# Attention output computed transposed for two query tiles at a time, in a hybrid decoder block

## The chip, the cores and the metric

The kernel runs on one core of one Trainium2 chip. The metric is the device time of one execution in microseconds (us); less is better. The engines' names are those of the profile: PE is TensorE (PEld its weight loads), DVE is VectorE, ACT is ScalarE, POOL is GpSimd, and SP is the sync engine, whose queue issues every DMA here.

## What is computed

One decoder block for 1024 tokens of width 1024, in float32. A normed input is projected; two kinds of attention with heads of width 64 run on the projections; their outputs are projected, gated and summed, projected again and added to the input; then comes a squared-ReLU MLP of width 4096 and a last norm. The part that matters:

```python
# 8 "fox" heads, causal over all 1024 keys, F = cumsum(log_sigmoid(fa + b))
s = q @ k.T * scale + F_q - F_k            # masked above the diagonal
oa = softmax(s) @ v
# 12 dilated heads: groups of 4 with dilation 1, 4, 16; blocks of own and previous keys
m = max(s); p = exp(s - m); denom = sum(p); lse = m + log(denom)
o_g = (p / denom) @ v
ob = sum_g softmax_g(lse)[g] * o_g         # mixture over the three groups
mixed = sigmoid(ga) * (oa @ w_branch_a) + sigmoid(gb) * (ob @ w_branch_b)
```

## The kernel before

Every float32 product is split: an operand is stored as a rounded part ("hi") and the rest ("lo", by a DVE subtraction), and two or three matmuls in the type fp32r are summed. All five engines run programs of their own, in an order written out by hand, and meet at semaphores.

**Units and steps.** After a start of 71 us the attention runs in ten units of two heads: `N_DIL` = 6 dilated units (two for each dilation), then `N_FOX` = 4 fox units. A unit has `STEPS` = 16 steps, numbered G in all: eight query tiles of 128 tokens times the unit's two heads (head `s % 2`, tile `s // 2`). The number of key tiles n of a step is 1 or 2 in a dilated unit (all 1 with dilation 16) and i + 1 in fox tile i, so 1 to 8. Between the two kinds lies the mixture of the dilated groups ("the join", L989 to L1027), and after the last unit come the branch projections, the gates and the MLP, which no longer concern the change except at their start.

**PE's step G** (`mixer_steps`, L962) is: `scores(G)` (L892, queries stationary, keys moving, both parts of q, a bank of up to four key tiles at a time); a third of the step's share of the next unit's input projections (`project_part`, L882; 128 x 512 matmuls, 144 in a unit as a rule, 96 in the first and last fox unit); `transposes(G - 1)` of the probabilities (L919, one for a key tile); the rest of the projections; `out_transpose` every second step (L931); and `values(G - 2)` (L938). In `values` a transposed tile of probabilities, 128 keys by 128 queries, is stationary, and 128 columns of values (64 hi, 64 lo) move. There are two matmuls for a key tile, since the probabilities have two parts. The result has queries on partitions; the half from the values' lo part is added, both are divided by the row sum, and the two heads' results lie side by side in `o_nat` until PE transposes them.

**DVE's step G** (L1835): `outs(G - 3)` (L1807), `maxes(G)` (L1783, adds the bias and takes the row maximum of the scores in PSUM), one job of the side work, `probs_lo(G - 1)` (L1794), `inverses(G - 1)` (L1802, a reciprocal), `q_tile(G + 2)` (L1765, two instructions), in step 1 of a unit `values_lo`, then the other jobs (splitting of weights, rotary embedding, `k_stack`).

**ACT's step G** (L1358): evacuation of a finished projection when there is one, `out_store` every second step (L1345, waits for `out_transpose`), `out_part(G - 3)` (L1337), `q_tile(G + 2)` (L1300, two instructions), `exps(G)` (L1321), `probs_hi(G - 1)` (L1329), then now and then a weight split or `k_stack`.

`values(G)` waits with `after(pe, on_done, G)` until DVE has read the result of the step before, since both lie in one bank. `scores(G)` waits for the queries of step G, which DVE makes two steps earlier (three buffers):

```python
pe.wait_ge(q_lo, 2 * G + 2)                 # L900, in scores(G)
after(pe, exp_done, G - 1)                  # L901
after(pe, on_done, G)                       # L943, in values(G)
if G < last and G + 2 < STEPS * MIX:        # L1848, in DVE's step G
    q_tile(G + 2)
```

**The join** needs the log of the row sums: ACT takes Ln of them (L1408), DVE subtracts the stored negative maxima (L1869), PE transposes the result to rows and, when ACT and DVE have put the tokens in natural order (L1409, L1871), back again (L997, L1003). DVE and ACT form the weights of the mixture (L1873 to L1888).

**SP** issues DMAs in order (L572 to L589): weight chunks, each behind a wait for its buffer, and the biases of the fox heads, broadcast from a row in DRAM to 128 partitions (L559).

Of the kernel before, what the change touches and what calls it, by code (L numbers as in the profile page):

```python
# [32 lines left out]
P = 128  # L33
# [25 lines left out]
PRIME = 1  # L59
STEPS = 16  # L60
MIX = N_DIL + N_FOX
# [92 lines left out]
def column(G):  # L154

    t, s = divmod(G, STEPS)
    if t >= N_DIL:
        return G
    return (((t // 2) * 8 + s // 2) * 2 + t % 2) * 2 + s % 2
# [14 lines left out]
def tiles_of(G):  # L174
    return key_tiles(G // STEPS, G % STEPS // 2)

# [11 lines left out]
def tile_tokens(ap, t, i):  # L188

    d = dil_of(t)  # L190
    if d in (None, 1):
        return ap[:, i * P:(i + 1) * P]
    v = ap.rearrange("p (l r) -> p r l", r=d)
    if d == 4:
        return v[:, i // 2, (i % 2) * P:(i % 2 + 1) * P]
    return v[:, 2 * i:2 * i + 2, :]


def tile_view(ap, t):

    return ap.rearrange("p (r l) -> p r l", r=2) if dil_of(t) == 16 else ap
# [20 lines left out]
def build(nc, x, g_attn, w_in, b_forget, w_branch, w_out, g_mlp, w_up, w_down, g_final, rope, f_rows, x_mid, hidden, out):  # L222
# [8 lines left out]
    with ExitStack() as ctx:  # L231
# [19 lines left out]

        up_b = [at(f"up_b{j}", [P, 2, 4, HALF], F32R, 64 + 16 * j) for j in range(3)]
# [23 lines left out]
        o_nat = sb("o_nat", [P, 2, P], F32)  # L276
        o_part = sb("o_part", [P, 2, HD], F32)
        negmax = sb("negmax", [P, STEPS * MIX], F32)
        rowsum = sb("rowsum", [P, STEPS * MIX], F32)
        rowinv = sb("rowinv", [P, STEPS * MIX], F32)  # L280
# [13 lines left out]
        v_nat = work[:, 4 * 1024:6 * 1024].rearrange("p (t h s d) -> p t h s d", t=8, h=2, s=2)  # L294
        q_st = work[:, 6144:6912].rearrange("p (b s c) -> p b s c", b=3, s=2)
        pt = work[:, 8 * 1024:12 * 1024].rearrange("p (b s c) -> p b s c", b=2, s=2)
# [13 lines left out]
        def ot_bank(i):  # L310

            return PS[1][:, HALF:HALF + P] if i < 8 * N_DIL else pso[:, 256:256 + P]

        def score_bias(G, n):

            t, s = divmod(G, STEPS)
            if t >= N_DIL:
                return fbias[t % 2][:, s % 2, 0:n * P]
# [4 lines left out]
        lse_nat = tmp[:, 6, 0:96].rearrange("p (g c) -> p g c", g=3)  # L323
        top = tmp[:, 6, 96:128]
        lrow = [tmp[0:4, 0, :], tmp[0:4, 1, :], tmp[0:4, 3, :]]
# [4 lines left out]
        def probs(G):  # L330

            if G < STEPS * N_DIL:
                return tmp[:, 6, (G % 2) * 256:(G % 2 + 1) * 256]
# [2018 lines left out]
```

## Time and profile before

| | us |
|---|---|
| median of 3 runs (1696.52 to 1700.22) | 1698.19 |
| the profiled execution's own time | 1698.49 |
| its span, first to last instruction | 1696.7 |
| six dilated units, 71 to 394 | 323 |
| the join, 394 to 425 | 31 |
| four fox units, 425 to 710 | 285 |
| everything after, 710 to the end | 986 |
| PE busy, share of the span | 94% |

The profiled execution lies 0.3 us above the median, and 1.8 us of it are outside the span. Busy time counts the union of an engine's instructions; the ends of matmuls are modelled, so the start of one matmul to the start of the next is the better price of it.

### The profile page before, as it was taken

The page shows a single profiled execution, that of the slowest core. Times are in us where ns is not written, and L with a number is a line of the kernel's source. Part 1 is how long each engine was busy: PE and PEld are TensorE (multiplying, and loading weights), DVE is VectorE, ACT ScalarE, POOL GpSimd, SP SyncE. Part 2 cuts the span into 40 slices and gives each one's busy share as a digit, 9 for nine tenths or more (in the row PEclk, how much of TensorE's full clock was granted, in tenths as well). Part 3 has the DMA queues.
Part 4 walks back from the last instruction along what each step waited for, and adds up shares of the span by engine and source line. Part 5 has one row for each costly group of instructions (what it writes and reads, how often), then busy time and mean ns, then how long its engine had stood idle before and what let it go on. Part 6 is the DMA issues. An engine that isn't in the chain of part 4 may idle for free. (4 is left out here: it accounts for less than half of the span.)

```text
span 1696.7 us, 22852 instructions
## 1 busy us (share of the span) xinstructions
PE 1592.8 (94%) x7832; PEld 1305.4 (77%) x7832; DVE 1114.5 (66%) x2167; ACT 831.1 (49%) x1715; POOL 4.1 (0%) x20
## 2 busy tenths in 40 slices
PE   5998998898799999999999999999999889999997
PEld 5777777675688887788888887888888667777786
DVE  5688788875666666622213667666666777777776
ACT  6566777783556666611113445344333444444441
POOL 0000000000000000000000000000000000000000
PEclk9999999999899999999999999999999999999998
DMA  5210110010010200011112533444444783444412
GB/s 174 87 38 26 26 38 26 26 38 13 14 50 14 63 26 10 16 53 47 49 53 71 149 101 92 157 154 143 153 165 156 238 283 135 153 137 137 143 38 100
DMA packets 160828, 152.45 MB, mean 90 GB/s; under 512 B 6856, under 2 KB 126664, under 8 KB 160592
## 3 DMA queue, kind: packets, MB, share of 16 engines
q1 hardware_dynamic: 160720, 151.06, 27.9%
q8 instruction: 61, 1.00, 0.2%
q14 instruction: 47, 0.39, 0.1%
HBM read 113.25 MB, written 37.78 MB: 89 GB/s over the span
## 5 line engine op out<-in xcount | busy, mean ns | idle before, releaser
L877 PE MATMUL ps<-hspl,wsp 128*128 128x512 f32 x1536 | 426.0, 411 | 8.3 <-ACT tmp L1290 6.7
L877 PEld LDWEIGHTS ps<-hspl,wsp 128*128 128x128 f32 x1536 | 268.0, 191 | 54.9 <-ACT tmp L1290 8.5
L1170 PE MATMUL ps<-dn_b,a_hi 128*128 128x512 f32 x896 | 279.6, 393 | 19.6 <-DVE keep L1957 13.9
L833 PE MATMUL ps<-hspl,wsp 128*128 128x512 f32 x960 | 223.2, 393 | 0.6 <-ACT keep L1356 0.6
L1170 PEld LDWEIGHTS ps<-dn_b,a_hi 128*128 128x128 f32 x896 | 167.8, 189 | 61.3 <-issue 26.1
L833 PEld LDWEIGHTS ps<-hspl,wsp 128*128 128x128 f32 x960 | 181.6, 190 | 38.5 <-issue 0.8
L1170 PE MATMUL ps<-dn_b,a_lo 128*128 128x512 f32 x448 | 175.7, 392 | 0.0
L1798 DVE TENSOR_TENSOR work<-ps,work 128x128 fp32r<-128x128 f32 (+3 forms) x192 | 84.4, 454 | 102.7 <-ACT work L1334 100.3
L949 PEld LDWEIGHTS ps<-work 128*128 128x128 f32 x856 | 112.6, 192 | 47.6 <-issue 37.6
L1326 ACT ACTIVATE tmp<-ps,negmax 128x128 f32<-128x128 f32 (+7 forms) x160 | 87.5, 547 | 122.8 <-DVE negmax L1791 121.0
L949 PE MATMUL ps<-work 128*128 128x128 f32 x856 | 122.9, 276 | 21.1 <-DVE o_nat L1813 20.0
L1957 DVE TENSOR_TENSOR keep<-keep,ps 128x512 f32<-128x512 f32 (+1 forms) x144 | 101.5, 713 | 38.3 <-PE ps L1170 23.6
L1170 PE MATMUL ps<-up_b,a_hi 128*128 128x512 f32 x384 | 119.6, 393 | 3.7 <-DVE up_b L1957 2.6
L1309 ACT ACTIVATE work<-tmp 64x128 fp32r<-64x128 f32 x320 | 113.3, 354 | 5.9
L1770 DVE SCALAR_TENSOR_TENSOR work<-tmp,work 64x128 fp32r<-64x128 f32 x320 | 101.5, 317 | 9.3 <-ACT work L1309 1.8
L1546 ACT ACTIVATE keep<-keep 128x512 f32<-128x512 f32 x64 | 40.5, 633 | 125.9 <-DVE keep L2129 42.8
L1170 PEld LDWEIGHTS ps<-dn_b,a_lo 128*128 128x128 f32 x448 | 84.7, 189 | 18.0
L916 PE MATMUL ps<-work 128*128 128x256 f32 (+3 forms) x384 | 89.2, 327 | 3.1 <-issue 2.1
L1957 DVE TENSOR_TENSOR dn_b<-dn_raw,dn_b 128x1024 fp32r<-128x1024 f32 x56 | 67.2, 1221 | 37.1 <-ACT dn_b L1562 37.1
L1948 DVE TENSOR_TENSOR wsp<-raw,wsp 128x1024 fp32r<-128x1024 f32 x18 | 22.0, 1223 | 105.8 <-ACT wsp L1454 105.8
L1993 DVE TENSOR_TENSOR a_lo<-a_raw,a_hi 128x1024 fp32r<-128x1024 f32 (+1 forms) x66 | 81.3, 1234 | 11.1 <-ACT a_hi L1512 10.9
L1170 PEld LDWEIGHTS ps<-up_b,a_hi 128*128 128x128 f32 x384 | 72.6, 190 | 19.7 <-DVE up_b L1957 3.1
(202 smaller groups left out, 2486.2 us busy)
## 6 DMA issues: line engine op xcount, KB each, us to landing
hidden<-keep SPq DMA_DIRECT2D x112, 256.0 KB, 2.2
dn_raw<-hidden SPq DMA_DIRECT2D x56, 512.0 KB, 6.0
raw<-in_w_in SPq DMA_DIRECT2D x47, 512.0 KB, 3.8
a_raw<-in_w_up SPq DMA_DIRECT2D x36, 256.0 KB, 3.1
a_raw<-in_w_down SPq DMA_DIRECT2D x32, 256.0 KB, 3.0
spare<-in_w_down SPq DMA_DIRECT2D x32, 256.0 KB, 4.6
spare<-in_w_up SPq DMA_DIRECT2D x28, 256.0 KB, 3.1
keep<-in_x SPq DMA_DIRECT2D x8, 512.0 KB, 7.1
```

The lines of the kernel that those rows point to most:

```text
L833: ins = pe.matmul(ps[:, cols], w(wp, k), mv(mp, k)[:, cols], start=(k == 0 and n == 0), stop=(k == ks - 1 and n == 2))
L877: ins = pe.matmul(psp(u, g), wsp[c % 2][:, wp, k * P:(k + 1) * P], hspl[:, mp, k, cols], start=(n == 0), stop=(n == 23), skip_group_check= ...
L916: ins = pe.matmul(oo, lt, rh, start=(m == 0), stop=(m == len(ops) - 1), skip_group_check=True)
L949: ins = pe.matmul(o, pt[:, G % 2, part, n * P:(n + 1) * P], v_nat[:, j, s % 2, :, :].rearrange("p s d -> p (s d)"), start=(part == 0 and n ...
L1170: ins = pe.matmul(o, a_part(n, j, wp, k), b_block(n, j, mp, k), start=(first and k == 0 and m == 0), stop=(k == ks - 1 and m == 2), skip_g ...
L1309: act.activation(tile_view(q_st[dst:dst + 64, G % 3, 0, :], t), tile_tokens(q_raw(t)[row:row + 64], t, s // 2), ACT.Copy, scale=-QSCALE).t ...
L1326: act.activation(probs(G)[:, 0:n * P], psc[G % 2][:, 0:n * P], ACT.Exp, bias=negmax[:, c:c + 1], scale=-1.0, accum_out=rowsum[:, c:c + 1]) ...
L1546: act.activation(u, u, ACT.Square).then_inc(signal, 1)
L1770: dve.scalar_tensor_tensor(out=tile_view(q_st[dst:dst + 64, G % 3, 1, :], t), in0=tile_tokens(q_raw(t)[row:row + 64], t, s // 2), scalar=- ...
L1798: dve.tensor_tensor(pt[:, G % 2, 1, a * P:b * P], PS[2][:, (u % 2) * HALF:(u % 2) * HALF + (b - a) * P], pt[:, G % 2, 0, a * P:b * P].bitc ...
L1957: return dve.tensor_tensor(out, a, b, op)
L1993: dve.tensor_tensor(a_lo_t[q % 2][b][:], src[:], a_hi_t[q % 2][b][:].bitcast(F32), ALU.subtract).then_inc(a_lo, 1)
```

## The change

The steps of a unit are ordered anew: `query_tile(s)` is `2 * (s // 4) + s % 2` and `head_of(s)` is `s // 2 % 2`, so that steps 2B and 2B + 1 are two neighbouring query tiles of one head, a block B (eight in a unit). The values become stationary (128 keys by 64 hi and 64 lo columns) and the probabilities of both tiles move, 256 columns where both tiles use a key tile and 128 where only one does. The result has the head's width on partitions, so `out_transpose` and `out_store` are gone, and DVE writes the sum of the two halves to its place. It isn't divided by the row sum. In the dilated units the weights of the mixture are formed from maxima and row sums without Ln (`mix_e`, `mix_r`); in the fox units a unit's 16 columns of reciprocals are transposed, stored to a new DRAM tensor `r_rows`, read back broadcast to 64 partitions for each head (`inv_wide`, in the buffer of the raw values), and DVE multiplies the whole unit's output once (`normalise`). `values(B)` runs at the end of PE's step 2B + 3. Queries are made in blocks of 256 columns, two ACT and two DVE instructions for two steps, in two buffers. `scores(2B)` waits for `q_lo` of both halves, the second of which DVE makes in step 2B - 1. Outputs have two banks in the dilated units and one in the fox units.

```diff
-    if t >= N_DIL:
-        return G
-    return (((t // 2) * 8 + s // 2) * 2 + t % 2) * 2 + s % 2
+def query_tile(s):
+
+    return 2 * (s // 4) + s % 2
+
+
+def head_of(s):
+
+    return s // 2 % 2
+
+
+def block_keys(B):
+
+    t, b = divmod(B, BLOCKS)
+    keys = [[j for j, _ in key_tiles(t, b // 2 * 2 + e)] for e in range(2)]
+    both = [j for j in keys[0] if j in keys[1]]
+    order = [(j, (0, 1)) for j in both]
+    order += [(j, (e,)) for e in range(2) for j in keys[e] if j not in both]
+    return min(keys[0] + keys[1]), order
 
 
...
+                             inv_rows[0:STEPS, :]).then_inc(inv_stored, 16)
+                sp.wait_ge(inv_stored, 16 * (f + 1))
+                sp.wait_ge(vt_done, 2 * min(N_DIL + f + 2, MIX))
+                for h in range(2):
+                    sp.dma_start(inv_wide[h * HD:(h + 1) * HD, :],
+                                 r_rows[2 * f + h:2 * f + h + 1, :].broadcast_to((HD, S))).then_inc(inv_in, 16)
+
             for i in range(4):
...
-                pe.wait_ge(q_lo, 2 * G + 2)
+                pe.wait_ge(q_lo, 2 * (G // 2) + 2)
                 after(pe, exp_done, G - 1)
+                query = q_st(G // 2)[:, :, G % 2 * P:(G % 2 + 1) * P]
                 ps = psc[G % 2]
...
+            def inverse_rows(f):
+
+                pe.wait_ge(inv_done, f + 1)
+                pe.wait_ge(on_done, BLOCKS * (N_DIL + f + 1) - 1)
+                pe.transpose(inv_bank, rowinv[:, f * STEPS:(f + 1) * STEPS], ident[:])
+
+            def values(B):
+                t, b = divmod(B, BLOCKS)
+                pe.wait_ge(pt_lo, units_before(2 * B + 2))
                 pe.wait_ge(v_lo, 2 * t + 2)
-                after(pe, on_done, G)
-                if t >= N_DIL:
-                    pe.wait_ge(ote_done, (G - 1) // 2)
-                o = pso[:, (s % 2) * P:(s % 2 + 1) * P]
-                for part in range(2):
-                    for n, (j, _) in enumerate(tiles):
-                        ins = pe.matmul(o, pt[:, G % 2, part, n * P:(n + 1) * P],
-                                        v_nat[:, j, s % 2, :, :].rearrange("p s d -> p (s d)"),
-                                        start=(part == 0 and n == 0), stop=(part == 1 and n == len(tiles) - 1))
+                after(pe, on_done, B if t >= N_DIL else B - 1)
+                base, keys = block_keys(B)
+                o = o_bank(B)
+                for n, (j, es) in enumerate(keys):
+                    cols = slice(es[0] * P, (es[-1] + 1) * P)
+                    for part in range(2):
+                        moving = pt(B, part)[:, j - base, es[0]:es[-1] + 1, :].rearrange("p e c -> p (e c)")
+                        ins = pe.matmul(o[:, cols], v_nat[:, j, 2 * (b % 2):2 * (b % 2) + 2, :].rearrange("p a d -> p (a d)"),
+                                        moving, start=(part == 0 and (n == 0 or len(keys[0][1]) == 1)),
+                                        stop=(part == 1 and n == len(keys) - 1), skip_group_check=True)
                 ins.then_inc(pv_done, 1)
...
-                    late = G if first else G - 1
-                    if late % 2 == 0 and late - 4 >= first:
-                        out_transpose((late - 4) // 2)
-                    if first <= G - 2 < last:
-                        values(G - 2)
+                    if G % 2 and first <= G - 3 < last:
+                        if G % STEPS == 1 and first:
+                            inverse_rows(G // STEPS - N_DIL - 1)
+                        values((G - 3) // 2)
                     if G % STEPS == 1 and G < last:
...
+            def query_hi(B, n):
+
+                t, b = divmod(B, BLOCKS)
+                if n == 0:
+                    act.wait_ge(raw_out, 6 * t + 4)
+                    if t < N_DIL:
+                        act.wait_ge(roped, 16 * t + 16)
+                    after(act, qk_done, 2 * B - 2)
+                row = 64 * (b % 2)
+                dst = row if n == 0 else 64 - row
+                act.activation(pair_view(q_st(B)[dst:dst + 64, 0, :], t), pair_tokens(q_raw(t)[row:row + 64], t, b // 2),
+                               ACT.Copy, scale=-QSCALE).then_inc(q_hi, 1)
...
+            def inverse_rows(f):
+
+                act.wait_ge(pv_done, BLOCKS * (N_DIL + f + 1))
+                after(act, inv_stored, 16 * f)
+                act.copy(inv_rows[0:STEPS, :], inv_bank).then_inc(inv_out, 1)
+
+            def out_part(B):
+
+                row = 64 * (B % 2)
+                act.wait_ge(pv_done, B + 1)
+                after(act, on_done, B - 1)
+                act.copy(o_part[row:row + 64, :], o_bank(B)[64 - row:P - row, :]).then_inc(op_done, 1)
...
-                    late = G if first else G - 1
-                    if late % 2 and first <= late - 5 < last:
-                        out_store((late - 5) // 2)
-                    if first <= G - 3 < last:
-                        out_part(G - 3)
-                    if G < last and G + 2 < STEPS * MIX:
-                        q_tile(G + 2)
+                    if G % 2 == 0 and first <= G - 4 < last:
+                        if s == 2 and first:
+                            inverse_rows(t - N_DIL - 1)
+                        out_part((G - 4) // 2)
+                    if G < last and G // 2 + 1 < BLOCKS * MIX:
+                        query_hi(G // 2 + 1, G % 2)
                     if G < last:
                         exps(G)
...
-            act.activation(rowsum[:, 0:96], rowsum[:, 0:96], ACT.Ln).then_inc(ln_ok, 1)
+            act.activation(mix_e, mix_e, ACT.Exp).then_inc(lexp_ok, 1)
...
+            def query_lo(B, n):
+                t, b = divmod(B, BLOCKS)
+                row = 64 * (b % 2)
+                dst = row if n == 0 else 64 - row
+                dve.wait_ge(q_hi, 2 * B + n + 1)
+                dve.scalar_tensor_tensor(out=pair_view(q_st(B)[dst:dst + 64, 1, :], t),
+                                         in0=pair_tokens(q_raw(t)[row:row + 64], t, b // 2), scalar=-QSCALE,
...
+            def inverses(f):
+                dve.wait_ge(exp_done, STEPS * (N_DIL + f + 1))
+                cols = slice(f * STEPS, (f + 1) * STEPS)
+                dve.reciprocal(rowinv[:, cols], fox_stat[:, 1, cols]).then_inc(inv_done, 1)
+
+            def outs(B):
+                t, b = divmod(B, BLOCKS)
+                row = 64 * (b % 2)
+                dst = og[:, t // 2, (t % 2) * 1024:(t % 2 + 1) * 1024] if t < N_DIL else keep[:, (t - N_DIL) * 1024:(t - N_DIL + 1) * 1024]
+                dve.wait_ge(op_done, B + 1)
+                dve.tensor_tensor(pair_tokens(dst[row:row + 64], t, b // 2), pair_view(o_bank(B)[row:row + 64, :], t),
+                                  pair_view(o_part[row:row + 64, :], t), ALU.add).then_inc(on_done, 1)
+
+            def normalise(f):
+                dve.wait_ge(inv_in, 32 * (f + 1))
+                dve.wait_ge(on_done, BLOCKS * (N_DIL + f + 1))
+                o = keep[:, f * 1024:(f + 1) * 1024]
+                dve.tensor_tensor(o, o, inv_wide, ALU.mult).then_inc(norm_ok, 1)
...
+                if t > N_DIL and s == 11:
+                    jobs.append(lambda: normalise(t - N_DIL - 1))
...
-                    if first <= G - 3 < last:
-                        outs(G - 3)
+                    if G % 2 == 0 and first <= G - 4 < last:
+                        outs((G - 4) // 2)
...
-                        inverses(G - 1)
-                    if G < last and G + 2 < STEPS * MIX:
-                        q_tile(G + 2)
+                        if first and G > first and s == 0:
+                            inverses(t - N_DIL - 1)
+                    if G < last and G // 2 + 1 < BLOCKS * MIX:
+                        query_lo(G // 2 + 1, G % 2)
...
+            link(dve.tensor_tensor(mix_r, mix_e, sum_nat, ALU.mult))
+            link(dve.tensor_tensor(top, mix_r[:, 0, :], mix_r[:, 1, :], ALU.add))
+            link(dve.tensor_tensor(top, top, mix_r[:, 2, :], ALU.add))
...
 
-            for k in range(6):
+            for n, k in enumerate(BR_ORDER):
                 src = keep[:, k * 1024:(k + 1) * 1024] if k < 4 else ob[:, (k - 4) * 1024:(k - 3) * 1024]
-                dve.wait_ge(br_hi, k + 1)
+                if k == N_FOX - 1:
+                    normalise(k)
```

## Rows read from the trace of the kernel before

**Rows 1.** The page's first part: busy time of the engines.
```profile
PE 1592.8 (94%) x7832; PEld 1305.4 (77%) x7832; DVE 1114.5 (66%) x2167; ACT 831.1 (49%) x1715; POOL 4.1 (0%) x20
```
**Rows 2.** By stage: window, length, busy PE, PEld, DVE, ACT, POOL, granted clock, DMA share, GB/s.
```profile
71.00:394.00 323.00, 294.05 (x1576) 234.53 (x1575) 257.16 (x832) 232.15 (x705) 0.00 (x0) 0.99 0.11 30
425.00:710.00 285.00, 267.32 (x1664) 225.57 (x1662) 181.35 (x515) 176.68 (x487) 0.00 (x0) 0.96 0.10 28
...
568.00:639.00 71.00, 69.83 (x440) 59.47 (x438) 45.47 (x130) 45.77 (x125) 0.00 (x0) 1.00 0.15 38
639.00:710.00 71.00, 65.21 (x430) 54.55 (x428) 42.51 (x128) 41.63 (x121) 0.00 (x0) 0.99 0.05 14
```
**Rows 3.** Waits from 71 to 394 us: who waited for whom, total us, times, longest.
```profile
PE ps L949 <- DVE o_nat L1813: 18.4, 27, 1.7
```
**Rows 4.** Timeline of PE in a fox unit: start, us, instruction.
```profile
622.51 2.09 PE L877 MATMUL ps<-hspl,wsp 128*128 128x512 f32 x8
624.44 1.45 PE L949 MATMUL ps<-work 128*128 128x128 f32 x12
625.73 1.14 PE L916 MATMUL ps<-work 128*128 128x512 f32 x4
```
**Rows 5.** Timeline of PE in a dilated unit: two 128 x 256 matmuls, then the second alone.
```profile
129.99 0.48 PE L916 MATMUL ps<-work 128*128 128x256 f32 x2
...
130.19 0.28 PE L916 MATMUL ps<-work 128*128 128x256 f32 x1
130.31 0.40 PE L877 MATMUL ps<-hspl,wsp 128*128 128x512 f32 x1
```
**Rows 6.** Groups of instructions by line and shape, 71 to 710 us: xcount | busy us, mean ns.
```profile
L1309 ACT ACTIVATE work<-tmp 64x128 fp32r<-64x128 f32 x316 | 112.0, 355 | 5.8
L1770 DVE SCALAR_TENSOR_TENSOR work<-tmp,work 64x128 fp32r<-64x128 f32 x316 | 100.3, 317 | 8.1 <-ACT work L1309 0.7
L1342 ACT ACTIVATE o_part<-ps,rowinv 128x64 f32<-128x64 f32 x160 | 51.9, 324 | 17.2 <-PE ps L949 16.2
L1813 DVE SCALAR_TENSOR_TENSOR o_nat<-ps,rowinv,o_part 128x64 f32<-128x64 f32 x160 | 45.0, 281 | 39.3 <-ACT o_part L1342 37.3
L1356 ACT COPY keep<-ps 128x128 f32<-128x128 f32 x80 | 25.7, 321 | 26.9 <-PE ps L949 24.9 <-PE ps L936 1.6
L1798 DVE TENSOR_TENSOR work<-ps,work 128x256 fp32r<-128x256 f32 x60 | 25.4, 423 | 18.6 <-ACT work L1334 18.1
L1805 DVE RECIPROCAL rowinv<-rowsum 128x1 f32<-128x1 f32 x160 | 24.5, 153 | 0.0
L1334 ACT CAST work<-ps 128x256 fp32r<-128x256 f32 x60 | 21.9, 365 | 0.0
L1791 DVE CUSTOM_DVE_ANT_0 ps<-ps,dil_bias 128x256 f32<-128x256 f32 x44 | 18.6, 423 | 0.0
L1326 ACT ACTIVATE tmp<-ps,negmax 128x256 f32<-128x256 f32 x52 | 24.7, 474 | 38.4 <-DVE negmax L1791 37.5
```
**Rows 7.** Timeline at the end of the last fox unit, two steps with eight key tiles.
```profile
694.34 1.22 DVE L1791 CUSTOM_DVE_ANT_0 ps<-ps,fbias 128x1024 f32<-128x1024 f32 x1
...
698.69 1.23 DVE L1791 CUSTOM_DVE_ANT_0 ps<-ps,fbias 128x1024 f32<-128x1024 f32 x1
...
710.44 13.71 PE L833 MATMUL ps<-hspl,wsp 128*128 128x512 f32 x48 [0.56 <-ACT keep L1356]
```
**Rows 8.** Timeline of the end of the dilated units and the join.
```profile
390.60 0.28 DVE L1798 TENSOR_TENSOR work<-ps,work 128x128 fp32r<-128x128 f32 x1
...
395.88 2.78 PE L997 MATMUL ps<-ident,rowsum 128*4 128x128 f32 x24 [0.49 <-DVE rowsum L1869]
...
404.76 1.28 ACT L1412 ACT_TABLE_LOAD   x1
```
**Rows 9.** Timeline of SP's queue: a row tensor stored to DRAM and read back broadcast.
```profile
56.58 0.48 SPq L581 DMA_DIRECT2D f_rows<-keep  x1
60.16 1.76 SPq L559 DMA_DIRECT2D fbias<-f_rows  x4
```

More of the change, by code:

```diff
@@ L174, in tiles_of @@
 def tiles_of(G):
-    return key_tiles(G // STEPS, G % STEPS // 2)
+    return key_tiles(G // STEPS, query_tile(G % STEPS))
 def units_of(G):
@@ L321, in score_bias, with stat @@
             return dil_bias[:, 2 - n:2, :].rearrange("p a c -> p (a c)")
-        lse_nat = tmp[:, 6, 0:96].rearrange("p (g c) -> p g c", g=3)
-        top = tmp[:, 6, 96:128]
-        lrow = [tmp[0:4, 0, :], tmp[0:4, 1, :], tmp[0:4, 3, :]]
+        stat_nat = tmp[:, 1, 0:192].rearrange("p (w x c) -> p w x c", w=2, c=4)
+        neg_nat, sum_nat = (tmp[:, 1, 96 * w:96 * w + 96].rearrange("p (g c) -> p g c", g=3) for w in range(2))
+        mix_e = tmp[:, 1, 192:288].rearrange("p (g c) -> p g c", g=3)
+        mix_r = tmp[:, 1, 288:384].rearrange("p (g c) -> p g c", g=3)
+        top = tmp[:, 1, 384:416]
+        lrow = [tmp[0:8, 0, :], tmp[0:8, 1, :], tmp[0:8, 3, :]]
+        inv_wide = tmp[:, 5, :]
+        def stat(G, w):
+            t, s = divmod(G, STEPS)
+            if t >= N_DIL:
+                c = (t - N_DIL) * STEPS + head_of(s) * 8 + query_tile(s)
+                return fox_stat[:, w, c:c + 1]
+            c = t % 2 * 2 + head_of(s)
+            return dil_stat[:, t // 2 * 8 + query_tile(s), w, c:c + 1]
         def q_raw(t):
@@ L962, in mixer_steps @@
             def mixer_steps(first, last):
-                for G in range(first, last + 4):
+                for G in range(first, last + 2):
                     if G < last:
@@ L1274, in raw_evacuate @@
                 elif g == 2:
-                    after(act, q_lo, 2 * STEPS * (u - 1))
+                    after(act, q_lo, 2 * BLOCKS * (u - 1))
+                    if u == N_DIL + 1:
+                        act.wait_ge(comb_ok, 1)
                 elif g == 4:
                     after(act, vt_done, 2 * u)
+                    after(act, norm_ok, u - 1 - N_DIL)
                     if u < N_DIL:
@@ L1896, in _ @@
                 dst = ob[:, pair * 1024:(pair + 1) * 1024]
-                one = dst if g == 0 else tmp[:, 6, :]
+                one = dst if g == 0 else tmp[:, 3, :]
                 dve.tensor_tensor(one, PS[pair][:], og[:, g, pair * 1024:(pair + 1) * 1024], ALU.mult).then_inc(spr_out, 1)
```

241 lines of the change are left out of this document (102 added, 139 removed).

## The prediction

> **What bounds the kernel now.** The page's head comes first: PE is busy for 94% of the span, DVE for 66% and ACT for 49% [rows 1], so a matmul saved in a full stage is time saved. The division by stage comes next, because the change touches only 71 to 425 us and the start of what follows [rows 2]. In the third fox unit, 568 to 639 us, PE is busy 69.8 of 71 us: work bounds it. In the fourth, 639 to 710, with 96 projections in place of 144, it is 65.2 of 71. In the dilated units PE is busy only 294 of 323 us, and the waits show why: PE stood idle 18.4 us before `values`, in 27 waits, for DVE's `outs` of the step before [rows 3].
>
> **The price of a matmul** is read from starts. Twelve 128-column matmuls of `values` take 624.44 to 625.73, 0.108 us each; eight with 512 columns take 622.51 to 624.44, 0.24 us each [rows 4]. The columns fell to a quarter and the price only to 45%: at 128 columns something else than columns sets it. A matmul of 256 columns is followed after 0.12 us (130.19 to 130.31) [rows 5]. The first of these stretches lies in a unit with the granted clock 1.00 [rows 2], that is 2.4 GHz.
>
> **The change, part by part.**
>
> *Values on PE.* A key tile used by both tiles of a block costs four matmuls of 128 columns now, 0.43 us, and two of 256 later, 0.24: 0.19 saved. By `key_tiles` a head has 4 shared key tiles with dilation 1, 4 with dilation 4, none with 16, and 1 + 3 + 5 + 7 = 16 in fox: 32 in the dilated heads, 128 in the fox heads. That is 6.1 and 24.3 us. (Matmuls: 856 to 536.) The bounds: at worst 256 columns cost 2 x 0.108, and nothing is saved; at best they cost 0.108, and 0.21 is saved.
> *Output transposes.* 80 go. Each has 128 columns; 0.108, as above, is the bound above and nothing the bound below, since most stand behind a 512-column matmul that may hide the weight load. I take 0.06: 2.9 us of the dilated units, 1.9 of fox.
> *DVE, two steps.* Now four query instructions at 0.317, two `outs` at 0.281, two reciprocals at 0.153: 2.14 us [rows 6]. Later two queries of 64 x 256, bounded by 0.317 and twice that, and one sum. The nearest row is the 128 x 256 subtraction, 0.423; I take 0.45 and 0.42: 1.32. A step loses 0.41 us.
> *ACT, two steps.* Now 4 x 0.355 + 2 x 0.324 + 0.321 = 2.39. Later two queries, 0.36 to 0.71, and one copy like the 128 x 256 cast, 0.365 [rows 6]; with 0.47 for a query, 1.31. A step loses 0.54.
> *The wait before `values`.* It now needs outputs of one block earlier (fox) or two (dilated), read by DVE over half a step before. The 18.4 us go. What is late next is below.
> *The new wait.* `scores(2B)` needs the queries that DVE makes last in step 2B - 1, after `probs_lo(2B - 2)`; before there was a step to spare. Behind this wait stand all PE's projections and transposes, and DVE's next `maxes` waits for its scores. From the end of the scores of 2B - 1 with two key tiles: maximum 0.42 and exp 0.47 with 0.1 to 0.15 of delay behind each, `probs_hi` 0.37, `probs_lo` 0.42, queries 0.45 [rows 6], some 2.4 us, while PE has eight projections (1.93), transposes (0.2) and a block of values (0.7), 2.8. So it is covered in the dilated units, by 0.4 us; a DVE job of 0.7 in between is hidden beside exp and cast, but `k_stack` is not.
> *Dilated units:* -6.1 - 2.9 - 18.4 = -27. A check: ACT and DVE set the pace in most of the 80 steps of the first five units, and 80 x 0.41 = 33. Ends: -15, if half the wait returns as another, and -38, if all PE's idle 29 us go.
> *Fox units.* DVE's steps are a ring: maximum, exp, cast, `probs_lo`, queries, next maximum. With eight key tiles and no queries left to make it takes 694.34 to 698.69, 4.35 us [rows 7]. Without reciprocal and `outs` (about 0.25 net) and with one query instruction it is 4.5. At every even step the scores come on top, four matmuls, about 1.0, less the 0.42 of `outs` that fits in: a mean of 4.9. PE's own work there is scores 1.0, transposes 8 x 0.108, half a block's values 0.95 and twelve projections 2.9 where a unit has 144, 5.7 a step; with six projections, in a unit of 96, it is 4.2. So the two middle units are bound by PE still and save a quarter of 26.2 each, 6.6. In the first and the last the ring keeps large steps as they are, and I take 4 each. The last block's output needs one wait fewer for `outs` and no transpose: 2. Fox: -23. Ends: -12 (ring everywhere) and -30 (all of PE's saving, tail included).
> *The join.* From the last `probs_lo`, 390.60, to the first transpose of statistics at 395.88 lie two waits of `values`, a transpose, a store, a table load and Ln [rows 8]. Later: one block of values, copy, sum, beside eight projections of 1.9 us: 2.5 saved. The second table load of 1.28, at 404.76, goes as well, since exp stays loaded; a wider copy and `mix_r` add 0.4. Together -3; ends -1 and -6.
> *Row sums of fox.* `normalise` is a 1.2 us DVE job in step 11 of three units, beside PE's work; its DMAs have seven steps and more. If that cover is gone, `raw_evacuate` of the values waits in step 14. SP stands still meanwhile for the store's landing, before the next weight chunk, which has several steps of room. Only the last unit's is exposed. The store and read-back of the row tensor took 3.6 us to the next issue [rows 9]; two broadcasts of half the size follow, for which I estimate 4 to 5 us, since issuing four alone took 1.76. With ACT's copy, multiply, split and the weight split behind it, about 14 us after the last `values`. PE has its next 48 products, which took 13.3 us [rows 7], plus 1 for the last output. I take +1; ends 0 and +4.
>
> Sum: -27 - 3 - 23 + 1 = -52 against the profiled execution's 1698.5: 1646. The median of the runs shown is 0.3 lower, which changes nothing. 0.2% is 3.4 us, about what a measurement of this kernel can tell from no change.
>
> **Rivals.**
> *A, the ring binds.* The new wait and the order of DVE set the pace in most steps. For it: DVE is busy 257 of 323 us in the dilated units, and its steps have few gaps there. Against: PE is fuller than DVE in each stage [rows 2]. Then the dilated units gain 17, fox 12, the join 3: -32 and +1, 1667.
> *B, 256 columns cost 0.17.* The pair takes 129.99 to 130.31, so the first, behind a transpose, took 0.2 [rows 5], and a dearer case exists. A shared tile then saves 0.09, not 0.19: 16 us less, 1662.
> *C, pairing saves no PE time.* Columns count, not matmuls, and 256 cost twice 128, which is 0.216: 30 us less, 1676. This is what the change would be if it did not do what it says. Against it stand rows 4 and 5.
> The Trainium skill speaks for C: TensorE: Matmul & The Clock Gate, Back-to-back issue gap, has an isolated gap of N / 2.4 + 2.5 ns, 56 for 128 columns and 109 for 256. By it a shared tile costs 0.222 now and 0.218 later, and the whole pairing is worth 1 us. The trace disagrees at 128 columns, with 108 ns [rows 4]. The same page gives a weight load about 107 ns (LDWEIGHTS), which with rows 4 would make the load the bound.
> *D, the cover is better.* With less work on all three engines most of PE's idle time goes too: dilated -38, fox -28, join -4, end +1: 1629.
> *E, slower.* The wait of `scores(2B)` for `q_lo`, 80 times. It eats the gain of 52 at 0.65 us a block. With a strided query instruction at 0.6 and a rotary job of 0.69 that is not hidden, the chain of 2.4 becomes 3.3 to 3.6 against 2.8 of PE; 0.8 x 80 = 64 makes 1710. Against: most jobs stand behind the queries or beside exp.
>
> **Chances.** Forecast 0.62, A 0.16, B 0.08, C 0.03, D 0.06, E 0.05. The forecast's own spread, with the ends of its terms, is 1634 to 1658. The range takes in A and B and a part of D: 1628 to 1670. Faster 0.93, within 0.2% 0.02, slower 0.05.
>
> **What would show it.** The dilated units end after 296 us instead of 323, fox takes 262 instead of 285. `values` has 536 matmuls, those of 256 columns 0.12 us apart; 0.2 apart would be B or C. No PE wait on DVE stands before it. A wait of PE's scores on DVE's query line, over 10 us in all, means A, over 40 means E. After the last unit, a wait of PE between the 48 products and the branch products over 2 us puts the row sums wrong. PE's busy share falls in the last fox unit, not in the middle two. A granted clock well below 1.00 in a middle unit would make the prices above wrong too.

## The result, and the profile after

The changed kernel takes 1676.97 us (median of 4 runs, 1672.13 to 1678.25), the kernel before beside it 1697.36 (1696.13 to 1700.22): a ratio of 0.9872, 95% interval 0.9848 to 0.9896. It is 20 us faster. The forecast was 52, and 1676.97 lies 7 us above its range of 1628 to 1670. The profiled execution took 1677.7 us, with a span of 1675.9.

The page's first part, against [rows 1]:

```profile
PE 1552.0 (93%) x7436; PEld 1277.8 (76%) x7436; DVE 1094.3 (65%) x1775; ACT 782.0 (47%) x1396; POOL 4.1 (0%) x20
```

PE is busy for 41 us less than before, and the span is only 21 us shorter. So the work went as it should, and about half of it came back as waiting. Where is told best by the starts of the maxima on DVE, one in each of the 160 steps. The first starts at 71.7 us, and these are the distances in us:

| | 1st to 96th (dilated) | 96th to 97th (join) | 97th to 160th (fox) |
|---|---|---|---|
| before | 315.4 | 41.6 | 270.3 |
| after | 309.4 | 36.6 | 263.2 |
| gone | 6.0 | 5.0 | 7.1 |

What follows the last maximum is 3 us shorter, nearly all of it behind the attention. There the profiled executions of this document differ by up to 10 us (990 to 1000) whatever the edit, so these 3 us are not put down to the change. By stage, against [rows 2] (columns as there):

```profile
71.00:382.00 311.00, 277.09 (x1447) 228.61 (x1446) 242.11 (x587) 203.67 (x507) 0.00 (x0) 0.98 0.11 30
414.00:689.00 275.00, 241.03 (x1371) 199.60 (x1372) 173.02 (x364) 156.97 (x364) 0.00 (x0) 0.95 0.12 35
554.00:622.00 68.00, 63.73 (x373) 53.12 (x372) 43.81 (x94) 40.94 (x95) 0.00 (x0) 1.00 0.18 48
622.00:690.00 68.00, 57.12 (x337) 47.34 (x336) 40.86 (x89) 36.70 (x88) 0.00 (x0) 0.96 0.08 22
```

The third fox unit (third row) has lost 6 us of PE work, as foretold, but only 3 us of its length: PE, which was busy for 69.8 of 71 us, now stands idle for 4.3 of 68. The prediction had the busy share falling in the last fox unit alone; it fell in this middle one too. The granted clock is 1.00 here as before, so the prices of matmuls hold. The longest waits of the dilated units and of fox (engine line waited for: us in total, times, longest us) say for what:

```profile
ACT tmp L1391 <- DVE dil_stat L1848: 77.0, 84, 1.6
DVE work L1855 <- ACT work L1401: 34.0, 67, 1.1
PEld ps L982 <- DVE work L1828: 27.9, 25, 2.4
PE ps L982 <- DVE work L1828: 24.3, 23, 2.3
...
PE ps L982 <- DVE q_fox L1828: 17.5, 17, 2.6
```

Line 982 is `scores`, and L1828 the query difference on DVE. The 18.4 us ahead of `values` [rows 3] are down to 1.3, and 24.3 + 17.5 = 42 us of a new wait have come. The prediction had named this wait and taken it as covered. One of these waits, on PE and on DVE:

```profile
192.32 0.40 PE L982 MATMUL ps<-work 128*128 128x256 f32 x2
...
194.52 0.57 PE L1014 MATMUL ps<-work 128*128 128x256 f32 x4
196.11 0.44 PE L982 MATMUL ps<-work 128*128 128x128 f32 x2 [1.02 <-DVE work L1828]
```

```profile
192.15 0.42 DVE L1855 TENSOR_TENSOR work<-ps,work 128x256 fp32r<-128x256 f32 x1 [0.24 <-ACT work L1401]
192.60 0.62 DVE L1828 SCALAR_TENSOR_TENSOR work<-tmp,work 64x256 fp32r<-64x256 f32 x1
193.25 0.69 DVE L1809 TENSOR_TENSOR tmp<-tmp 128x512 f32<-128x512 f32 x1
193.86 0.42 DVE L1848 CUSTOM_DVE_ANT_0 ps<-ps,dil_bias 128x256 f32<-128x256 f32 x1
194.21 0.14 DVE L1848 DVE_READ_ACCUMULATOR2_ANT dil_stat<- 128x1 f32 x1
194.21 0.69 DVE L1811 TENSOR_TENSOR tmp<-tmp 128x512 f32<-128x512 f32 x1
195.13 0.29 DVE L1855 TENSOR_TENSOR work<-ps,work 128x128 fp32r<-128x128 f32 x1 [0.24 <-ACT work L1401]
195.46 0.60 DVE L1828 SCALAR_TENSOR_TENSOR work<-tmp,work 64x256 fp32r<-64x256 f32 x1
```

The scores of the odd step end at 192.72, but their maximum starts only at 193.86, 1.14 us later: DVE has the query of the step before and a rotary job in hand. From the maximum to the end of the next query another 2.2 us pass. So the queries come 3.34 us after the scores, and PE, with 2.37 us of work in between, waits 1.02.

### The profile page after: what moved, and what is told of

Read it like the earlier page. It is cut to its first block and busy times, and to the rows that moved or that the text cites. A ratio compares the mean times of both kernels' runs of the same rounds, so it can differ in the third digit from the quotient of the medians.

```text
span 1675.9 us, 20825 instructions
## 1 busy us (share of the span) xinstructions
PE 1552.0 (93%) x7436; PEld 1277.8 (76%) x7436; DVE 1094.3 (65%) x1775; ACT 782.0 (47%) x1396; POOL 4.1 (0%) x20
## 5 line engine op out<-in xcount | busy, mean ns | idle before, releaser
L1233 PE MATMUL ps<-dn_b,a_hi 128*128 128x512 f32 x896 | 280.0, 394 | 17.5 <-DVE keep L2022 11.8
L1233 PEld LDWEIGHTS ps<-dn_b,a_hi 128*128 128x128 f32 x896 | 168.0, 189 | 59.3 <-issue 24.1
L2022 DVE TENSOR_TENSOR keep<-keep,ps 128x512 f32<-128x512 f32 (+1 forms) x144 | 101.5, 713 | 38.2 <-PE ps L1233 24.5
L1855 DVE TENSOR_TENSOR work<-ps,work 128x128 fp32r<-128x128 f32 (+3 forms) x144 | 59.1, 420 | 72.3 <-ACT work L1401 70.2
L1391 ACT ACTIVATE tmp<-ps,fox_stat 128x128 f32<-128x128 f32 (+3 forms) x64 | 47.5, 742 | 94.9 <-DVE fox_stat L1848 94.8
L993 PE MATMUL ps<-ident,tmp 128*128 128x128 f32 x428 | 75.7, 281 | 9.7 <-issue 7.1
L1580 ACT COPY ps<-ps 128x512 f32<-128x512 f32 x46 | 26.3, 571 | 123.8 <-PE ps L1233 118.4
L1233 PE MATMUL ps<-up_t4b,a_hi 128*128 128x512 f32 x256 | 80.1, 395 | 1.2 <-ACT keep L1600 1.2
L1233 PE MATMUL ps<-up_t,a_hi 128*128 128x512 f32 x256 | 79.1, 390 | 0.0
L993 PEld LDWEIGHTS ps<-ident,tmp 128*128 128x128 f32 x428 | 55.7, 144 | 29.7 <-issue 14.2
```

Source lines behind the costliest of these rows:

```text
L993: ins = pe.transpose(PS[2][:, (u % 2) * HALF + (k - a) * P:(u % 2) * HALF + (k - a + 1) * P], probs(G)[:, k * P:(k + 1) * P], ident[:])
L1233: ins = pe.matmul(o, a_part(n, j, wp, k), b_block(n, j, mp, k), start=(first and k == 0 and m == 0), stop=(k == ks - 1 and m == 2), skip_g ...
L1391: act.activation(probs(G)[:, 0:n * P], psc[G % 2][:, 0:n * P], ACT.Exp, bias=stat(G, 0), scale=-1.0, accum_out=stat(G, 1)).then_inc(exp_do ...
L1580: act.copy(s1[q] if q < 2 else bank_b(q), bank_a(q)).then_inc(s1_ok, 1)
L1855: dve.tensor_tensor(pt_tiles(G, 1, a, b), PS[2][:, (u % 2) * HALF:(u % 2) * HALF + (b - a) * P].rearrange("p (j c) -> p j c", c=P), pt_til ...
L2022: return dve.tensor_tensor(out, a, b, op)
```

## The experiments

Each is an edit of the changed kernel unless said otherwise. The distances between maxima, in us, for all:

| | dilated | join | fox |
|---|---|---|---|
| e1_query_first | 291.3 | 38.4 | 242.5 |
| e2_both_halves_even | 308.5 | 38.2 | 256.4 |
| e3_unpaired | 310.0 | 39.1 | 275.1 |
| e4_before_late_query | 359.5 | 44.5 | 291.9 |
| e5_query_first_unpaired | 294.0 | 36.8 | 261.5 |
| e6_before_query_first | 303.6 | 41.6 | 263.2 |
| e7_third_query_buffer | 301.2 | 38.1 | 262.5 |
| e8_query_first_third_buffer | 292.8 | 36.8 | 243.6 |
| e9_values_lo_late | 309.5 | 38.3 | 250.2 |
| e10_k_stack_late | 305.9 | 38.5 | 252.6 |
| e11_longer_query | 327.0 | 38.1 | 272.9 |
| e12_query_first_longer_query | 302.3 | 38.3 | 242.4 |

**e1_query_first** puts the query behind the maximum, into the time in which DVE waits for exp and cast:

```diff
                     if G < last:
                         maxes(G)
+                    if G < last and G // 2 + 1 < BLOCKS * MIX:
+                        query_lo(G // 2 + 1, G % 2)
                     for job in jobs[:1]:
                         job()
                     if first <= G - 1 < last:
                         probs_lo(G - 1)
...
-                    if G < last and G // 2 + 1 < BLOCKS * MIX:
-                        query_lo(G // 2 + 1, G % 2)
```

> The changed kernel with one order of DVE's step changed: query_lo stands right behind maxes, ahead of the side job and of probs_lo. Nothing is left out. Theory W (the wait of scores(2B) for queries made behind probs_lo, and with it DVE's ring, ate the gain): PE's idle time in front of scores falls from about 42 us (24.3 dilated, 17.5 fox) to under 8, the query instruction of 0.4 to 0.6 us goes into a gap in which DVE waited for exp and cast, and the time falls by 25 to 40 us, to 1637 to 1652. Rival D (DVE and ACT have too much work for the step, wherever the queries stand): the idle time turns up in front of transposes and values, and the time stays within 6 us of 1677. Rival M (the moving pairs or the low granted clock are what costs): 1677 too, with the wait in front of scores gone.

Measured: 1639.65 us (1638.16 to 1641.05), ratio to before 0.9653 (0.9635 to 0.967). It is 37 us below the changed kernel, beats both kernels, and nothing tried later beats it. The wait in question, in the dilated units:

```profile
PE ps L982 <- DVE work L1828: 8.5, 10, 1.7
```

In fox it is no longer among the thirteen longest. The order of two instructions was worth more than the change.

**e2_both_halves_even** makes both halves of a block's queries in the even step (ACT and DVE), where they were made one in each:

```diff
-                    if G < last and G // 2 + 1 < BLOCKS * MIX:
-                        query_lo(G // 2 + 1, G % 2)
+                    if G < last and G % 2 == 0 and G // 2 + 1 < BLOCKS * MIX:
+                        query_lo(G // 2 + 1, 0)
+                        query_lo(G // 2 + 1, 1)
```

> The changed kernel with both halves of a block's queries made in the even step 2B (ACT and DVE), one step ahead of where the second half was made. The place behind probs_lo stays, so the wait is loosened by a step and DVE's ring keeps its length. Theory W: the idle time in front of scores falls under 10 us as well, but DVE's serial work per two steps is the same, so that less is won than with the queries moved into DVE's gap: 8 to 25 us below 1677. Rival D: 1671 to 1683.

Measured: 1670.29 us (1669.31 to 1675.17), ratio 0.9842 (0.9819 to 0.9865). That lies between the ranges of the two theories. The wait of `scores` for queries is gone, and it brings only 7 us: in the dilated units the distance from an even step's maximum to the next grew from 2.51 to 3.19 us in the mean (from an odd one it fell from 4.02 to 3.30), and PE waits elsewhere, its transposes for exp. So room alone isn't it; the length of DVE's chain fits as the rest.

```profile
DVE work L1856 <- ACT work L1401: 73.4, 107, 1.9
PEld ps L993 <- ACT tmp L1391: 37.8, 39, 2.3
```

**e3_unpaired** and **e5_query_first_unpaired** take the pairing back, in the changed kernel and in e1, with all else kept:

```diff
-                    for part in range(2):
-                        moving = pt(B, part)[:, j - base, es[0]:es[-1] + 1, :]...
+                    for e in es:
+                        for part in range(2):
+                            moving = pt(B, part)[:, j - base, e, :]
```

> The changed kernel with 128 moving columns everywhere: a shared key tile takes four matmuls again, 856 in place of 536. Nothing is left out. By the price in the trace (256 columns 0.118 us, 128 columns 0.11) this adds some 32 us of PE work, 26 of it in the fox units. Theory W: PE waits about 0.5 us a block for the queries, with half of that work standing in front of the wait, so that only a part of it reaches the end: 8 to 22 us above 1677. Rival P (PE's work sets the pace and the pairing saved all of its 31 us): 28 to 34 us above.

> The changed kernel with the query differences right behind the maxima (as in e1_query_first, 1639.65 us), and beside that every values matmul with 128 columns again (856 instead of 536). In e3 the same unpairing cost only 14 us where PE stood waiting anyway. Theory W (the wait for the queries had swallowed half of what pairing saves, and is gone here): 25 to 32 us slower than e1, 1665 to 1671, near the 30.4 of the prediction's term. Rival R (the DVE ring still sets most steps, whatever the place of the queries): no more than in e3, 8 to 18 slower, 1648 to 1657.

Measured: e3 1691.16 us (1686.05 to 1698.38), ratio 0.9961 (0.994 to 0.9982); e5 1665.33 (1663.56 to 1665.93), ratio 0.9807 (0.9787 to 0.9827). Pairing is worth some 14 us where PE waits for queries (the ten runs of e3 scatter over 12) and 26 where it doesn't. By stage, where it doesn't: 2.7 us dilated and 19.0 in fox, of 6.1 and 24.3 foretold. The rest of the 26 lies behind the attention, where e5 had the clock at half for 35 us and e1 for 20; between the first and the last maximum it was the other way, 14 us and 24.

**e4_before_late_query** gives the kernel before the lack of room that the change has: `q_tile(G + 1)` and `q_tile(G + 2)` both in the odd step, on ACT and DVE.

```diff
-                    if G < last and G + 2 < STEPS * MIX:
-                        q_tile(G + 2)
+                    for x in (G + 1, G + 2) if G % 2 and G < last else ():
+                        if x < STEPS * MIX:
+                            q_tile(x)
```

> The kernel before, with one thing of the change alone: ACT and DVE make q_tile(G + 1) and q_tile(G + 2) in the odd steps G, so that the even step's scores wait for queries made one step ahead, behind probs_lo, as in the changed kernel. Work and counts are those of before. Theory W: an idle time of PE in front of scores appears in the even steps, 20 to 50 us in all, and the time rises by 12 to 40 us over 1697. Rival D (the order alone costs nothing): within 4 us of 1697.

Measured: 1764.9 us (1759.65 to 1767.52), ratio 1.0384 (1.0358 to 1.0411). The wait is there (`scores` is L916), and the slowdown of 67 us is larger than either theory's number. A part of it is the clock, which was granted at half for 65 us between the first and the last maximum, against 27 in the kernel before; at most 19 us can come from that. The wait:

```profile
PE ps L916 <- DVE work L1771: 62.2, 52, 2.7
```

Here four query instructions stand in one step, where the change has one, so this shows that the wait can arise, not its size in the change.

**e6_before_query_first** asks what e1's edit does to the kernel before, which has room:

```diff
                         maxes(G)
+                    if G < last and G + 2 < STEPS * MIX:
+                        q_tile(G + 2)
                     for job in jobs[:1]:
...
-                    if G < last and G + 2 < STEPS * MIX:
-                        q_tile(G + 2)
```

> The kernel before with its DVE query instructions moved right behind the maxima of their step, ahead of the side job and of probs_lo; nothing else. It asks whether e1's 37 us came from the wait of the scores or from a shorter DVE chain that any kernel would gain by. Theory W (before had a step to spare for its queries, so moving them serves no wait; the chain had its gaps filled by outs and reciprocals): within 5 us of the kernel before, 1693 to 1701. Rival R (queries in the shadow of exp and cast shorten DVE's chain in every step, wait or no wait): 12 to 35 us faster, 1662 to 1685.

Measured: 1679.06 us (1678.51 to 1681.83), ratio 0.9897 (0.9876 to 0.9918). My expectation missed: 19 us go where PE didn't wait for queries. If the order is worth the same in the changed kernel, 19 of e1's 37 us have nothing to do with the change and 18 belong to it; no run shows that the two add up in this way. With the queries first on both sides, the change is worth 1679.06 - 1639.65 = 39 us; with them last, 20.

**e7_third_query_buffer** restores the room and leaves the order alone, in the dilated heads (a third buffer, each query a step earlier except at the start of a head). **e8_query_first_third_buffer** adds it to e1.

```diff
-            return (q_dil if B < BLOCKS * N_DIL else q_fox)[:, B % 2]
+            return q_dil[:, B % 3] if B < BLOCKS * N_DIL else q_fox[:, B % 2]
...
-                        query_lo(G // 2 + 1, G % 2)
+                        for q in queries_of(G):
+                            query_lo(*q)
```

> The changed kernel with the order of its instructions within a step kept, but a third query buffer in the dilated heads, and each query made one step earlier there (so scores of an even step has again a step to spare, as before the change). Fox is as it was. Theory W (the missing step of room is what costs): the 24 us of PE's scores waiting on the query line between 71 and 415 us fall to under 5, and 12 to 22 us go: 1655 to 1665. Rival R (the place of the query instructions in DVE's chain costs, not the room): the wait moves to another line and 0 to 5 us go, 1672 to 1677.

> e1_query_first with the third query buffer of e7 in the dilated heads: both remedies at once. W and R alike: in e1 8.5 us of PE's scores waiting on the query line are left in the dilated heads; they go, and 2 to 8 us with them, 1632 to 1638. If the two remedies were independent and each worth its full amount, it would be 15 or more.

Measured: e7 1668.36 us (1664.98 to 1669.67), ratio 0.9824 (0.9801 to 0.9847); e8 1642.06 (1639.79 to 1643.43), 0.967 (0.9649 to 0.9691). Both miss: e7 lies between its two theories, and e8 gains nothing where 2 to 8 us were expected. In e7 the query wait is gone from the dilated units' list and 8.2 us with it; 18 us of another wait have come, of PE's transposes for ACT's exp, which waits for the maximum:

```profile
ACT tmp L1402 <- DVE dil_stat L1861: 85.1, 84, 2.3
...
PE ps L1004 <- ACT tmp L1402: 18.3, 27, 1.7
```

So the wait of `scores` and the length of DVE's chain are two limits close together. Taking away the first uncovers the second, after 8 of 24 us. In e1 the order relieves both, and there a third buffer adds nothing (2 us slower, within the scatter): e1's last 8.5 us of the query wait go, and PE's transposes wait for exp for 15.0 us where they did for 4.7 in e1.

**e11_longer_query** and **e12_query_first_longer_query** price DVE's time in the two orders: one more instruction of 64 x 128 ahead of each query, into a scratch tensor.

```diff
                 dve.wait_ge(q_hi, 2 * B + n + 1)
+                dve.scalar_tensor_tensor(out=half(pair_view(dup_out[dst:dst + 64, :], t)),
+                                         in0=half(pair_tokens(q_raw(t)[row:row + 64], t, b // 2)), scalar=-QSCALE, ...
```

> The changed kernel, order kept, with one more DVE instruction of 64x128 (the query difference of half the columns, into a scratch tensor, 0.3 us) ahead of each query difference, so last in DVE's step: it prices an error of length of the query instruction, which I had put 0.13 us a step too short. If DVE's chain sets the pace in nearly every step: 160 x 0.3 = 48 us slower, and at least 35 (1712 to 1725). If PE sets it in most: under 20 slower (under 1697).

> The same additional instruction in e1_query_first (1639.65), where it lies behind the maxima, in the time in which DVE waits for exp and cast. If the shadow of exp and cast (0.47 + 0.15 + 0.37, less the query's 0.5) still has 0.3 us of room: 0 to 12 slower, 1640 to 1652. If not: 25 to 48 slower, 1665 to 1688.

Measured: e11 1706.18 us (1702.78 to 1707.91), ratio 1.0048 (1.0033 to 1.0063), 29 above the changed kernel and between the two numbers; e12 1648.13 (1646.93 to 1651.47), 0.9715 (0.9693 to 0.9737), 8 above e1, as expected. What was added, in e11 (line, operation, shapes, xcount | busy us, mean ns):

```profile
L1833 DVE SCALAR_TENSOR_TENSOR dup_out<-tmp,work 64x128 f32<-64x128 f32 x94 | 32.3, 343 | 2.8 <-ACT work L1378 0.5
L1833 DVE SCALAR_TENSOR_TENSOR dup_out<-tmp,q_fox 64x128 f32<-64x128 f32 x61 | 17.3, 283 | 1.4
```

With the queries last, 32.3 us in the dilated units cost 17.6, and 17.3 in fox cost 9.7: 0.55 us for each. With the queries first, 11.0 and nothing.

**e9_values_lo_late** and **e10_k_stack_late** tried to improve e1 by the same rule. The second diff is e10's, on top of e9.

```diff
+                    if s == 2 and G < last:
+                        values_lo(t)
                     for job in jobs[:1]:
...
-                    if s == 1 and G < last:
-                        values_lo(t)
```

```diff
-                    for job in jobs[:1]:
+                    ahead = 0 if s in (9, 15) and t + 1 < MIX else 1
+                    for job in jobs[:ahead]:
...
-                    for job in jobs[1:]:
+                    for job in jobs[ahead:]:
```

> e1_query_first with DVE's values_lo (the low half of a head's values, which waits for PE's value transposes at the end of step 1) moved from the end of step 1 to behind maxes and query of step 2. In e1 the step from the second to the third maximum takes 5.4 us in every dilated head and 5.8 to 6.7 in fox, the neighbours 2 to 4: maxes(2) is queued behind that wait. If so, about 1 us a head goes, 1627 to 1634. Rival: those steps are long by PE's eight transposes and ACT's copies, and nothing goes: 1637 to 1641.

> e9 with the k_stack job (2.0 us of DVE) in steps 9 and 15 behind probs_lo instead of ahead of it. By the rule that what PE waits for (probs_lo, queries) goes first: the steps from the tenth maximum, 5.8 us in e1, get shorter by up to 1, 2 to 8 us in all below e9. Rival: the 2.0 us stand in DVE's way on either side of probs_lo, within 2 us of e9.

Measured: e9 1661.58 us (1658.41 to 1666.76), ratio 0.979 (0.9761 to 0.982); e10 1662.98 (1660.47 to 1667.12), 0.9798 (0.9772 to 0.9824). e9 is 22 us slower than e1, against both theories, and e10 doesn't differ from it; the steps from the tenth maximum that it was to shorten take 6.0 to 6.2 us in the second to fifth unit, for 5.8 to 6.0 in e1. Step 2 of e9's second unit, on DVE and on PE:

```profile
129.90 0.43 DVE L1869 TENSOR_TENSOR keep<-ps,o_part 64x256 f32<-64x256 f32 x1 [2.98 <-ACT o_part L1416]
130.36 0.30 DVE L1848 CUSTOM_DVE_ANT_0 ps<-ps,dil_bias 128x128 f32<-128x128 f32 x1
130.68 0.08 DVE L1848 DVE_READ_ACCUMULATOR2_ANT dil_stat<- 128x1 f32 x1
130.68 0.41 DVE L1828 SCALAR_TENSOR_TENSOR work<-tmp,work 64x256 fp32r<-64x256 f32 x1
131.02 1.28 DVE L1836 TENSOR_TENSOR work<-ps,work 128x512 fp32r<-128x512 f32 x2
```

```profile
128.82 0.68 PE L942 MATMUL ps<-hspl,wsp 128*128 128x512 f32 x2
132.40 0.66 PE L993 MATMUL ps<-ident,tmp 128*128 128x128 f32 x2 [2.90 <-issue]
132.71 2.91 PE L942 MATMUL ps<-hspl,wsp 128*128 128x512 f32 x6
```

I had overlooked `outs`, at the head of DVE's step 2: it waits for ACT's `out_part`, which stands behind the copies of the values, so in the dilated units DVE's maximum comes only 0.5 us sooner (5.0 after the one before it, for 5.5 in e1), and `values_lo` (L1836) now ends later, at 132.30. PE's `transposes(1)` need it by the program; they start at 132.40, after 2.9 us in which PE stood idle. Then something else is seen: the six projections behind the pause take 2.91 us, in e1 the same six take 1.64. The granted clock, in e9 (columns as in rows 2):

```profile
128.00:132.00 4.00, 1.50 (x12) 1.06 (x10) 2.05 (x6) 2.31 (x6) 0.00 (x0) 0.95 0.00 0
132.00:136.00 4.00, 3.60 (x11) 3.06 (x12) 0.72 (x2) 1.66 (x3) 0.00 (x0) 0.50 0.00 0
```

The pause is paid a second time by the slow clock. Between the first and the last maximum the clock was granted at half for 51 us in e9, for 24 in e1. These 27 us more can make at most 14 of the 22, if PE had work in all of them; the rest fits the pauses themselves.

## Why the prediction was wrong

**The step that failed** is the new wait: "So it is covered in the dilated units, by 0.4 us", from a chain of 2.4 us against 2.8 of PE's work. In the step shown above the chain takes 3.34 and PE's work 2.37. The chain is 0.94 us longer, and the 1.14 between scores and maximum are more than the whole of it (from the maximum on it takes 2.20, with a `probs_lo` of one key tile). The sum didn't have them: it began with the maximum as soon as the scores were there, while DVE was still at the last instructions of the step before, the query and a job. The query itself takes 0.60 there for my 0.45. Rival E had this chain, 3.3 to 3.6, from nearly the same causes. On PE the eight projections and a transpose took 1.96 (192.56 to 194.52) for my 2.13 and `values` 0.57 for 0.7, and the first 0.16 of it lay beside the end of the scores. e1 shows what the place of the queries is worth: with them moved, the dilated units end 24.1 us sooner than before, where 27 were forecast, and fox 27.8, where 23 were. But the kernel before gains by the same move (e6), 11.8 and 7.1 us. With the queries first on both sides the change brings 12.3 us in the dilated units, 3.2 in the join and 20.7 in fox. So with the queries first fox and the join come out about as forecast, and the dilated units don't.

**Dilated -27** came out as -6. Its parts on PE held: the wait ahead of `values` went (18.4 to 1.3), and PE's busy time between the first and the last maximum of these units fell from 288.5 to 275.4 us. But a second step failed here, adding the whole of that wait to the gain. From e6 to e1 the wait goes from 14.6 us to 1.3 and PE's busy time falls by 11.3, and these units get only 12.3 us shorter: PE stands idle for 19.3 us in e6 and for 18.6 in e1, now ahead of scores and transposes. e8, without any query wait, is no shorter. That DVE's chain is what keeps this idle time is argued, not shown. The sizes on DVE did not hold: the query took 0.541 us in the mean for my 0.45 and `outs` 0.495 for 0.42, where a tensor is read or written with a stride:

```profile
L1376 ACT ACTIVATE work<-tmp 64x256 fp32r<-64x256 f32 x94 | 54.4, 579 | 2.3
L1828 DVE SCALAR_TENSOR_TENSOR work<-tmp,work 64x256 fp32r<-64x256 f32 x94 | 50.8, 541 | 2.7 <-ACT work L1376 0.5
...
L1828 DVE SCALAR_TENSOR_TENSOR q_fox<-tmp,q_fox 64x256 fp32r<-64x256 f32 x64 | 26.7, 416 | 1.5
```

That is 94 x 0.09 + 48 x 0.075 = 12 us more on DVE, and at the 0.55 of e11 some 7 us of the 21 that are missing. This is an estimate. The check "80 x 0.41 = 33" failed more deeply: it took a shorter sum of instructions for a shorter step. Query, `outs` and reciprocals could partly lie where DVE waited anyway, and e6 shows how much of the step's length was order: 11.8 us of the dilated units in the kernel before.

**Fox -23** came out as -7.1 between the maxima. By unit, from the first maximum to the next unit's first (the last: to its own last):

| fox unit | before | after | e6 | e1 |
|---|---|---|---|---|
| first | 68.7 | 68.1 | 65.0 | 60.6 |
| second | 70.6 | 68.3 | 71.2 | 65.2 |
| third | 71.3 | 67.8 | 71.1 | 65.2 |
| fourth | 59.7 | 59.0 | 55.9 | 51.5 |

"So the two middle units are bound by PE still and save a quarter of 26.2 each, 6.6" gave 2.3 and 3.5 in the changed kernel and 5.4 and 6.1 in e1, 6.0 and 5.9 from e6 to e1: the sum of PE's work was right and the condition, a PE that never waits, was not met. "I take 4 each" for the first and last unit gave 0.6 and 0.7. There PE has the fewest projections to lay beside the chain. e1 is 8 us shorter than before in each, of which the order alone gives 3.7 and 3.8 (e6); from e6 to e1 it is 4.4 each, about what I took. The 2 us for the last block's output gave 0.1: the last block's 16 matmuls ran 0.21 us apart, at the half clock, behind a pause of 1.72 us for the reciprocal of the row sums.

```profile
687.54 0.28 PE L1001 MATMUL ps<-ident,rowinv 128*16 128x128 f32 x1 [1.72 <-DVE rowinv L1862]
687.64 0.37 PE L1014 MATMUL ps<-pt_odd,work 128*128 128x256 f32 x1
687.84 0.39 PE L1014 MATMUL ps<-work 128*128 128x256 f32 x1
...
692.50 11.15 PE L898 MATMUL ps<-hspl,wsp 128*128 128x512 f32 x48 [1.40 <-DVE keep L1869]
703.84 1.42 PE L898 MATMUL ps<-work,wsp 128*128 128x512 f32 x5 [0.19 <-DVE wsp L1749]
```

**The row sums, +1,** were right in kind: the branch products wait 0.19 us behind the 48 products, so store, broadcasts and multiply are covered. **The join, -3,** gave 5.0.

**The price of a matmul** was right. At the full clock the 256-column matmuls of `values` follow each other after 0.12 us:

```profile
608.49 0.28 PE L1014 MATMUL ps<-pt_odd,work 128*128 128x256 f32 x1
608.60 0.28 PE L1014 MATMUL ps<-work 128*128 128x256 f32 x1
...
609.56 0.28 PE L1014 MATMUL ps<-work 128*128 128x256 f32 x1
```

0.119 (1.07 us over nine) against the forecast 0.12, and e5 puts the pairing at 26 us for 30. That buries rivals B and C, the second by what it said (pairing saves nothing); that its time, 1676, is the one measured is chance. The Trainium skill's rule (TensorE: Matmul & The Clock Gate, Back-to-back issue gap) gives, for isolated matmuls, 109 ns for 256 columns and 56 for 128. The trace agrees within a tenth at 256 and not at 128, where 108 were read [rows 4]. Of the rivals A and E, which rest on the new wait, were the nearest in kind. A's 1667 has gains of 17, 12 and 3 us where 6.0, 7.1 and 5.0 came. The prediction's own mark for E, over 40 us of PE's scores waiting on the query line, was passed (42), at 0.5 us a block; E's price of 0.8 a block was not reached, and the kernel got faster.

What stays open: how e1's gain of 37 us divides between the wait and DVE's chain in fox, where a third buffer wasn't tried, and how much of any version's time the clock's fall behind pauses makes: it was seen, but no run changed it by itself. It isn't where the missing 32 us went: between the first and the last maximum the clock was at half for 27 us in the kernel before and for 34 in the changed one, and 7 us more can cost at most 3.5.

## What to carry to other kernels

Where an edit removes a step of room from a buffer, write the producer's whole step down, from what it is doing when the consumer's input arrives, not from the moment that it could begin. Where a change removes a wait, don't book the whole of it before the next limit is priced. Then look at the order within the step: an instruction that another engine waits for belongs where its own engine waits anyway, here behind the maximum, in the time of exp and cast. Two orders of the same instructions differed by 37 us, more than the change brought, and a version should be judged in its best order (39 us here, 20 as written). Before moving a consumer back, look at what heads the queue ahead of it (e9).

## What the runs showed of the hardware

A pause of PE can cost twice. In e9, at one of 2.90 us, the granted clock fell, to 0.50 (1.2 GHz) from 132 to 136 us, and six 512-column matmuls took 2.91 us for 1.64. In the changed kernel the mean from 688 to 692 us is 0.59, behind a pause of 1.72 us. The query instruction of 64 x 256 takes about 0.60 us on DVE and 0.66 on ACT in the dilated units with dilation 4 and 16, where its operand is read with a stride, and 0.42 on both in the others and in fox.
